# Slope term and causal mask of an attention moved from the vector engine into products on TensorE

## The chip, the core and the metric

One core of one Trainium2 chip runs the kernel. The metric is the device time of one execution in microseconds. A core has five engines that run their own instruction streams and meet at semaphores: TensorE (PE in the profile, with its weight loads shown apart as PEld), the vector engine (DVE), the scalar engine (ACT), GpSimd (POOL) and SyncE (SP), which issues transfers. Products land in PSUM, eight banks of 128 partitions by 512 fp32 numbers; everything else lies in SBUF.

## The reference, cut to what matters

The program is two transformer blocks on 512 tokens. The change touches two of the attentions of the first block and one neighbour. All three have eight heads, and all see the causal past only:

```
slopes = [2 ** -(h + 1) for h in range(8)]              # the two sparse/window branches only
# kinds 0 and 1 (selected blocks, window): queries and keys of 64 numbers a head
s = q @ k.T * 64 ** -0.5 - slopes[h] * (t - j)           # t: query, j: key
# kind 2 (latent attention): queries and keys of 96 numbers a head, no slope
s = (q_nope @ k_nope.T + q_rope @ k_rope.T) * 96 ** -0.5
p = softmax(where(j <= t, s, -1e30)) ; o = p @ v
```

With 512 tokens, eight blocks of 64 and sixteen to be chosen, the selection takes every block, and the window of 512 covers the whole past. So kinds 0 and 1 are both plain causal attentions with a slope term, over different keys and values. A softmax doesn't change when a number is added to a whole row of its scores, and so the term may be written as slopes[h] * j plus any constant of the row.

## The kernel before, in words

The first block runs in stages: projections (to 101 us of the profiled span), preparation of the attention's operands and the compressed attention (to 173 us), the attention stage (173 to 346 us), merge and feed-forward (to about 1000 us). The second block follows; from 1275 us on it streams the experts' weights.

**The attention stage** is cut into 48 units (`UNITS`, line 1600). A unit is one block of 128 queries (i = 0..3, so that nk = 128 * (i + 1) keys are seen), one kind, and two heads, pr and pr + 4 (hh = 0, 1). Units come in pairs, a long one and a short one: in the first 24 units i = 3 and i = 0 alternate ("(3,0)"), in the last 24 units i = 2 and i = 1 ("(2,1)"). In each half, eight units are kind 0, then eight kind 1, then eight kind 2. Each pair thus has five blocks of 128 keys a head, whichever half it is in.

For each unit, in order:

- TensorE (`scores`, lines 1710 to 1723) multiplies queries and keys, in fp32, into two PSUM banks, one a head. For kinds 0 and 1 the two heads lie in rows 0 to 63 and 64 to 127 of the array, so that their two products run side by side (line 1722); kind 2 uses 96 rows (line 1719). It waits until the exponentials of the unit before last have freed the banks.
- DVE (`mask_max`, line 2135) adds slope and mask in PSUM. For kinds 0 and 1 it is one instruction a head over all nk columns (line 2145), with a table of distances in which the future is -1e30; for kind 2 one instruction adds the 128-column diagonal table to both heads (line 2141). One reduction gives the negated row maxima of both heads (line 2149).
- ACT (`exps`, line 1884) computes the exponential of each head with that maximum as bias, into SBUF, and sums it.
- TensorE (`turn_probs`, line 1733) turns the probabilities in 128x128 pieces; DVE copies the first head's to SBUF (line 2157), ACT the second head's (line 1893).
- TensorE (`values`, line 1746) multiplies them with the values, 64 columns at a time, in fp32.

TensorE's order is: scores(u+1), turn(u), values(u-1). When a group of four units is through, DVE scales and gathers its output (`combine`, lines 2162 to 2171), in its own order, between two masks.

An fp32 product runs as two records in the trace, each with its weight load. Operands written as fp32r, a rounded format, run as one.

Of the kernel before, what the change touches and what calls it, by code (L numbers as in the profile page):

```python
# [119 lines left out]
CSTS = [("ident", 128), ("eps", 1), ("ones", 128), ("diag", 128), ("alibi", 512), ("inv_freq", 16), ("row_ok", 1),  # L120
# [14 lines left out]
cs_tr_ev cs_pv cs_o at_s at_max at_exp at_tr at_ev_dve at_ev_act at_pv at_o mg_sig mg_ev up_conv up_dve  # L135
# [28 lines left out]
def build(nc, W, EX, x, cols, csts, cmp_tab, pos, grows, pT, fconst, fwout, decay, frow, out):  # L164
    ctx = ExitStack()
    with ctx:
# [114 lines left out]

        rows_split = ar_r(25312, 2048).rearrange("p (u w c) -> p u w c", u=2, w=2)
# [1321 lines left out]
        def _(pe):  # L1604
# [103 lines left out]
            pe.wait_ge(S["cs_o"], 1)  # L1708

            def scores(u):  # L1710
                i, kind, pr, w = UNITS[u]
                nk = (i + 1) * P
                if u >= 2:
                    pe.wait_ge(S["at_exp"], 2 * (u - 1))
                for hh in range(2):
                    h = pr + 4 * hh
                    dst = pb[:, 2 * (u % 2) + hh, 0:nk]
                    if kind == 2:
                        last = nc.tensor.matmul(dst, qTm[0:QK, h, i * P:(i + 1) * P], kTm[0:QK, h, 0:nk], start=True, stop=True)
                    else:  # L1720
                        r = slice((h // 4) * 64, (h // 4) * 64 + 64)
                        last = nc.tensor.matmul(dst, qT[r, h % 4, i * P:(i + 1) * P], kvT[r, 2 + kind, 0:nk], start=True, stop=True)  # L1722
                last.then_inc(S["at_s"], 1)
# [89 lines left out]
        def _(act):  # L1813
# [60 lines left out]
            nc.scalar.activation(Pc[:, :, :, 0:31], Pc[:, :, :, 0:31], ACT.Exp).then_inc(S["cs_exp"], 1)  # L1874

            def exps(u):
                i, kind, pr, w = UNITS[u]
                nk = (i + 1) * P
                act.wait_ge(S["at_max"], u + 1)
                for hh in range(2):  # L1880
                    if u >= 2:
# [112 lines left out]
        def _(dve):  # L1994
# [136 lines left out]
            alibi = cs("alibi")  # L2131
# [3 lines left out]
            def mask_max(u):  # L2135
# [3 lines left out]
                dve.wait_ge(S["at_s"], u + 1)  # L2139
                if kind == 2:  # L2140
                    L(nc.vector.tensor_tensor(pb[:, b:b + 2, nk - P:nk], pb[:, b:b + 2, nk - P:nk],
                                              cs("diag").unsqueeze(1).broadcast_to([P, 2, P]), ALU.add))
                else:
                    for hh in range(2):
                        ins = nc.vector.scalar_tensor_tensor(out=pb[:, b + hh, 0:nk], in0=alibi[:, 512 - nk:512],  # L2145
# [334 lines left out]
```

## Time and profile before

| | us |
|---|---|
| median of 3 runs | 1809.21 |
| lowest and highest of them | 1800.8, 1812.97 |
| the profiled execution, its own time | 1807.25 |
| its span in the profile | 1805.5 |
| TensorE busy in the span | 1533.8 (85%) |
| DVE busy | 636.9 (35%) |
| mean granted TensorE clock | 0.93 of full |
| attention stage, first scores to the next stage's first turn | 173.6 to 345.8 |

The profile is of one execution. A granted clock of 1.00 is TensorE's full 2.4 GHz, 0.50 is 1.2 GHz. A record of a product lasts until its last number has left the array, so records of products that follow closely overlap, and the distance from one start to the next is what a product costs in a dense queue.

### The profile page before, as it was taken

What the parts mean: (1) busy time and instruction counts of PE and PEld (TensorE: products, weight loads), DVE (VectorE), ACT (ScalarE), POOL (GpSimd) and SP (SyncE); (2) the same over time, 40 slices, a digit from 0 to 9 for tenths busy, and PEclk for the clock granted to TensorE, in tenths of its full rate; (3) what the DMA queues carried; (4) which work ended last, traced back from release to release, by engine and by line L of the source; (5) the groups of instructions that cost most, each with busy time, mean ns of one, the idle gap of its engine ahead of it and who ended that gap; (6) DMA issues with size and microseconds to landing.
All of it is one profiled execution on the core that took longest, in us unless ns stands there. A gap on an engine that the chain in (4) does not pass through costs nothing.

```text
span 1805.5 us, 18567 instructions
## 1 busy us (share of the span) xinstructions
PE 1533.8 (85%) x7176; PEld 1038.8 (58%) x7177; DVE 636.9 (35%) x968; ACT 466.4 (26%) x798; POOL 464.4 (26%) x272
## 2 busy tenths in 40 slices
PE   7976898899979999999997899896687777877871
PEld 5954576788767888878866666466332222222320
DVE  3244667712345333332143778654300000000003
ACT  4231334432233333321134333322000000000001
POOL 4420000144334444444423363521010000010001
PEclk9986888999999999999999899997799999999996
DMA  7320000033232332323323222127499999999983
GB/s 278 105 71 35 1 1 1 1 94 100 87 93 82 101 98 94 97 90 95 94 80 105 76 82 68 50 109 287 177 427 427 428 427 426 426 426 423 424 352 147
DMA packets 47045, 315.24 MB, mean 175 GB/s; under 512 B 7344, under 2 KB 7344, under 8 KB 34560
## 3 DMA queue, kind: packets, MB, share of 16 engines
q1 hardware_dynamic: 37296, 286.80, 41.3%
q0 software_dynamic: 9104, 25.39, 3.9%
q10 hardware_dynamic: 576, 2.10, 0.3%
q8 instruction: 47, 0.77, 0.2%
q14 instruction: 22, 0.18, 0.0%
HBM read 307.97 MB, written 14.68 MB: 179 GB/s over the span
## 4 chain that ended last, share of the span: by engine, by line
PE 60%; DMA 18%; DVE 14%; issue 3%; ACT 2%; POOL 1%; SPq 0%; POOLq 0%; ACTq 0%; DVEq 0%
PE banks L353 22%; DMA arena<-experts 17%; PE banks L383 10%; PE banks L920 8%; PE banks L1776 3%; PE banks L363 2%; PE banks L831 1%; PE banks L1746 1%; DVE st L2149 1%; PE banks L688 1%; PE banks L1733 1%; PE banks L689 1%; DVE banks L2145 1%; PE banks L1722 1%; DVE arena_r L1580 1%
## 5 line engine op out<-in xcount | busy, mean ns | idle before, releaser
L331 POOL TENSOR_TENSOR arena_r<-ring,arena_r 128x1024 fp32r<-128x1024 f32 x143 | 353.2, 2472 | 747.1 <-ACT arena_r L316 747.1
L353 PE MATMUL banks<-hT_r,arena_r 128*128 128x512 f32 x1216 | 391.9, 392 | 8.7 <-POOL arena_r L331 4.3
L920 PE MATMUL banks<-ring,arena 128*64 128x512 f32 x768 | 246.0, 626 | 65.2 <-DMA arena<-experts 45.1
L353 PE MATMUL banks<-arena_r 128*128 128x512 f32 x800 | 291.7, 389 | 0.0
L316 ACT ACTIVATE arena_r<-ring 128x1024 fp32r<-128x1024 f32 x143 | 151.1, 1059 | 519.6 <-PE banks L353 316.9
L353 PEld LDWEIGHTS banks<-hT_r,arena_r 128*128 128x128 f32 x1216 | 228.4, 188 | 67.4 <-issue 9.2
L920 PEld LDWEIGHTS banks<-ring,arena 128*64 128x64 f32 x768 | 80.6, 144 | 218.4 <-issue 161.0
L383 PE MATMUL banks<-arena_r 128*128 128x512 f32 x784 | 187.4, 393 | 3.6 <-POOL arena_r L331 3.6
L383 PEld LDWEIGHTS banks<-arena_r 128*128 128x128 f32 x784 | 147.2, 188 | 38.3 <-POOL arena_r L331 5.4
L353 PEld LDWEIGHTS banks<-arena_r 128*128 128x128 f32 x800 | 150.3, 188 | 30.8
L942 PE MATMUL banks<-arena 128*64 128x512 f32 x512 | 118.5, 617 | 19.4 <-DMA arena<-experts 13.9
L920 PE MATMUL banks<-arena 128*64 128x512 f32 x256 | 130.8, 670 | 0.0
L587 POOL DMA_INDIRECT back<-arena,at_out x16 | 16.3, 1017 | 441.5 <-DVE arena L1384 229.4
L1379 DVE TENSOR_TENSOR arena<-arena,banks 128x512 f32<-128x512 f32 x16 | 11.0, 688 | 300.1 <-PE banks L920 300.1
L942 PEld LDWEIGHTS banks<-arena 128*64 128x64 f32 x512 | 40.3, 141 | 87.3 <-issue 74.6
L2236 DVE SCALAR_TENSOR_TENSOR arena<-banks,colt,arena 128x511 f32<-128x511 f32 x44 | 33.0, 750 | 151.6 <-ACT arena L1937 151.6
L1884 ACT ACTIVATE arena<-banks,st 128x512 f32<-128x512 f32 (+3 forms) x96 | 49.8, 525 | 107.8 <-DVE st L2149 107.7
L1733 PE MATMUL banks<-cst,arena 128*128 128x128 f32 x240 | 46.6, 315 | 21.8 <-ACT arena L1884 13.5
L1558 PE MATMUL banks<-cst,arena 128*128 128x128 f32 x192 | 30.8, 329 | 40.0 <-DVE arena L1532 25.9
L1746 PE MATMUL banks<-arena 128*128 128x64 f32 x480 | 64.3, 286 | 0.0
L1384 DVE COPY arena<-banks 128x512 f32<-128x512 f32 x16 | 11.1, 692 | 150.6 <-PE banks L942 150.6
L1746 PEld LDWEIGHTS banks<-arena 128*128 128x128 f32 x480 | 63.4, 208 | 0.0
(391 smaller groups left out, 1816.0 us busy)
## 6 DMA issues: line engine op xcount, KB each, us to landing
arena<-experts SPq DMA_DIRECT2D x48, 2048.0 KB, 21.2
ring<-experts SPq DMA_DIRECT2D x48, 2048.0 KB, 18.1
ring<-stream SPq DMA_DIRECT2D x163, 512.0 KB, 3.5
rows<-arena POOLq DMA_DIRECT2D x8, 512.0 KB, 6.8
arena<-back POOLq DMA_DIRECT2D x8, 512.0 KB, 7.3
grow<-grows POOLq DMA_DIRECT2D x5, 512.0 KB, 4.6
resid<-x ACTq DMA_DIRECT2D x4, 512.0 KB, 5.4
out<-arena POOLq DMA_DIRECT2D x4, 512.0 KB, 3.0
```

Source lines behind the costliest of these rows:

```text
L316: nc.scalar.activation(parts(name, m)[:, 0, :], tile(tile_n), ACT.Copy).then_inc(S["w_high"], 1)
L331: nc.gpsimd.tensor_tensor(w[:, 1, :], tile(tile_n), plain(w[:, 0, :]), ALU.subtract).then_inc(S["w_low"], 1)
L353: last = nc.tensor.matmul(pb[:, bank, :], w[:, a, k * P:(k + 1) * P], b[:, k, :], start=(k == 0 and part == 0), stop=(k == ND - 1 and part ...
L363: last = nc.tensor.matmul(pb[:, bank0 + i, 0:width], a[:, k, i * P:(i + 1) * P], w[:, v, q * width:(q + 1) * width], start=(k == 0 and par ...
L383: last = nc.tensor.matmul(pb[:, 2 * i + h, :], u[row], w[:, v, h * 512:(h + 1) * 512], start=(k == 0 and part == 0), stop=(k == K - 1 and ...
L920: last = nc.tensor.matmul(pb[r, bank, :], XT[:, k, r], chunk(c + e)[:, k * 512:(k + 1) * 512], start=(k == 0), stop=(k == ND - 1))
L942: last = nc.tensor.matmul(pb[r, 3 + h, :], hbT[:, k, r], chunk(4 + e)[:, k * D + h * 512:k * D + (h + 1) * 512], start=(k == 0), stop=(k = ...
L1733: last = nc.tensor.transpose(pb[:, 4 + hh, kt * P:(kt + 1) * P], Pr[:, u % 2, hh, kt * P:(kt + 1) * P], ident)
L1746: last = nc.tensor.matmul(pb[:, 6 + w % 2, h * DH:(h + 1) * DH], PTs[:, u % 2, hh, kt * P:(kt + 1) * P], v, start=(kt == 0), stop=(kt == i))
L1776: last = nc.tensor.matmul(pb[:, b + 2 + w, :], tw[:, u, (4 * w + k) * P:(4 * w + k + 1) * P], src[:, k, :], start=(k == 0 and part == 0), ...
L1884: nc.scalar.activation(Pr[:, u % 2, hh, 0:nk], pb[:, 2 * (u % 2) + hh, 0:nk], ACT.Exp, bias=nm[:, u % 2, hh:hh + 1], accum_out=sums[:, w, ...
L2236: L(nc.vector.scalar_tensor_tensor(out=c[:, 1:T], in0=u[:, 0:T - 1], scalar=col("w_conv", 2 * NF + m), in1=c[:, 1:T], op0=ALU.mult, op1=AL ...
```

## The change

Mask and slope are now part of the products that fill the banks. Four tables are rounded to fp32r by ACT after the compressed attention's exponential (`ident_r`, `diag_r`, `steps_r`, `slopes_r`). For kinds 0 and 1 a one-row product of the head's slope, repeated over 128 columns, with the key positions (0 for the last key, -1 for the one before) adds the slope term over all nk columns. For all kinds the product of the identity with the diagonal table adds the mask to the last 128 columns. DVE loses its additions, and its reduction becomes one a head, with a semaphore count a head from the product to the exponential.

```diff
--- before.py
+++ after.py
@@ -117,7 +117,7 @@
 N_COLS = _at
 
 
-CSTS = [("ident", 128), ("eps", 1), ("ones", 128), ("diag", 128), ("alibi", 512), ("inv_freq", 16), ("row_ok", 1),
+CSTS = [("ident", 128), ("eps", 1), ("ones", 128), ("diag", 128), ("steps", 512), ("slopes", 8), ("inv_freq", 16), ("row_ok", 1),
         ("giota", 4), ("eiota", 32), ("tri", 128), ("iota", 128), ("choice", 8), ("empty", 1), ("ecolumn", 32), ("erow", 32)]
 CST = {}
 _at = 0
@@ -132,7 +132,7 @@
 w_used w_high w_low rows_low hT_low oT_low h_high h_back cols_in ident_in x_in0 x_in1 x_in2 x_in3 tab_in g_in decay_in out_st
 dve_chain proj_fm_ev proj_mla_ev proj_v_ev cmp_blocks cmp_gelu cmp_kv cmp_ready ang_ready sin_ready mla_ms
 mla_rt mla_norm mla_tr mla_tr_ev mla_up q_ev kv_ev q_raw qk_tr qk_ev_act qk_ev_dve cs_mm cs_max cs_exp cs_tr
-cs_tr_ev cs_pv cs_o at_s at_max at_exp at_tr at_ev_dve at_ev_act at_pv at_o mg_sig mg_ev up_conv up_dve
+cs_tr_ev cs_pv cs_o at_tab at_s at_max at_exp at_tr at_ev_dve at_ev_act at_pv at_o mg_sig mg_ev up_conv up_dve
 up_gelu up_g ple_mm ple_ev pg_mm pg_sig in2_lin in2_conv in2_f z_ready f_in flt_mm flt_act flt_dve
 mixed tf_mm tf_act prod_ready y_ready xz_ready combined yh_dve pool_chain hn_sq_f hn_sq_h hn_ms hn_rt hn_y
 wo2_mm wo2_x rt_lg rt_g rt_d rt_exp rows_st xg_zero slot_ready slot_mm sel_ready rank_mm counts_out
@@ -279,6 +279,7 @@
         def ar_r(off, n):
             return arena_r[:, off:off + n]
 
+        ident_r, diag_r, steps_r, slopes_r = ar_r(25312, P), ar_r(25440, P), ar_r(25568, T), ar_r(26080, HEADS)
         rows_split = ar_r(25312, 2048).rearrange("p (u w c) -> p u w c", u=2, w=2)
         up_low = ar_r(18432, ND * T).rearrange("p (k t) -> p k t", k=ND)
 
@@ -1706,21 +1707,27 @@
 
 
             pe.wait_ge(S["cs_o"], 1)
+            pe.wait_ge(S["at_tab"], 4)
 
             def scores(u):
                 i, kind, pr, w = UNITS[u]
                 nk = (i + 1) * P
                 if u >= 2:
                     pe.wait_ge(S["at_exp"], 2 * (u - 1))
+                dst = [pb[:, 2 * (u % 2) + hh, 0:nk] for hh in range(2)]
                 for hh in range(2):
                     h = pr + 4 * hh
-                    dst = pb[:, 2 * (u % 2) + hh, 0:nk]
+                    r = slice(64 * hh, 64 * hh + 64)
                     if kind == 2:
-                        last = nc.tensor.matmul(dst, qTm[0:QK, h, i * P:(i + 1) * P], kTm[0:QK, h, 0:nk], start=True, stop=True)
+                        nc.tensor.matmul(dst[hh], qTm[0:QK, h, i * P:(i + 1) * P], kTm[0:QK, h, 0:nk], start=True, stop=False)
                     else:
-                        r = slice((h // 4) * 64, (h // 4) * 64 + 64)
-                        last = nc.tensor.matmul(dst, qT[r, h % 4, i * P:(i + 1) * P], kvT[r, 2 + kind, 0:nk], start=True, stop=True)
-                last.then_inc(S["at_s"], 1)
+                        nc.tensor.matmul(dst[hh], qT[r, pr, i * P:(i + 1) * P], kvT[r, 2 + kind, 0:nk], start=True, stop=False)
+                for hh in range(2):
+                    h = pr + 4 * hh
+                    if kind < 2:
+                        nc.tensor.matmul(dst[hh], slopes_r[0:1, h:h + 1].broadcast_to([1, P]), steps_r[0:1, T - nk:T],
+                                         start=False, stop=False)
+                    nc.tensor.matmul(dst[hh][:, nk - P:nk], ident_r, diag_r, start=False, stop=True).then_inc(S["at_s"], 1)
 
             def turn_probs(u):
                 i, kind, pr, w = UNITS[u]
@@ -1872,12 +1879,14 @@
 
             act.wait_ge(S["cs_max"], 1)
             nc.scalar.activation(Pc[:, :, :, 0:31], Pc[:, :, :, 0:31], ACT.Exp).then_inc(S["cs_exp"], 1)
+            for dst, name in ((ident_r, "ident"), (diag_r, "diag"), (steps_r, "steps"), (slopes_r, "slopes")):
+                nc.scalar.activation(dst, cs(name), ACT.Copy).then_inc(S["at_tab"], 1)
 
             def exps(u):
                 i, kind, pr, w = UNITS[u]
                 nk = (i + 1) * P
-                act.wait_ge(S["at_max"], u + 1)
                 for hh in range(2):
+                    act.wait_ge(S["at_max"], 2 * u + hh + 1)
                     if u >= 2:
 
                         act.wait_ge(S["at_tr"], 2 * (u - 2) + hh + 1)
@@ -2128,7 +2137,6 @@
                                     fac.unsqueeze(2).broadcast_to([P, 32, DH]), ALU.mult).then_inc(S["cs_o"], 1)
             dve.wait_ge(S["cs_o"], 1)
 
-            alibi = cs("alibi")
             rinv = st[:, 428:436]
             otmp = junk[:, 0:512]
 
@@ -2136,18 +2144,10 @@
                 i, kind, pr, w = UNITS[u]
                 nk = (i + 1) * P
                 b = 2 * (u % 2)
-                dve.wait_ge(S["at_s"], u + 1)
-                if kind == 2:
-                    L(nc.vector.tensor_tensor(pb[:, b:b + 2, nk - P:nk], pb[:, b:b + 2, nk - P:nk],
-                                              cs("diag").unsqueeze(1).broadcast_to([P, 2, P]), ALU.add))
-                else:
-                    for hh in range(2):
-                        ins = nc.vector.scalar_tensor_tensor(out=pb[:, b + hh, 0:nk], in0=alibi[:, 512 - nk:512],
-                                                             scalar=SLOPES[pr + 4 * hh], in1=pb[:, b + hh, 0:nk],
-                                                             op0=ALU.mult, op1=ALU.add)
-                    L(ins)
-                nc.vector.tensor_reduce(nm[:, u % 2, :], pb[:, b:b + 2, 0:nk], AX.X, ALU.max, negate=True)\
-                    .then_inc(S["at_max"], 1)
+                for hh in range(2):
+                    dve.wait_ge(S["at_s"], 2 * u + hh + 1)
+                    nc.vector.tensor_reduce(nm[:, u % 2, hh:hh + 1], pb[:, b + hh, 0:nk], AX.X, ALU.max, negate=True)\
+                        .then_inc(S["at_max"], 1)
 
             def copy_turned(u):
                 nk = (UNITS[u][0] + 1) * P
@@ -2304,7 +2304,8 @@
     p = np.arange(P)
     c = {"ident": np.eye(P), "eps": np.full((P, 1), EPS), "ones": np.ones((P, P)), "diag": np.where(p[None, :] <= p[:, None], 0.0, NEG)}
     dist = p[:, None] - (np.arange(512)[None, :] - 384)
-    c["alibi"] = np.where(dist >= 0, -dist, NEG)
+    c["steps"] = np.broadcast_to(np.arange(T) - (T - 1), (P, T))
+    c["slopes"] = np.broadcast_to(np.array(SLOPES), (P, HEADS))
     inv = (np.float32(10000.0) ** (-np.arange(0, 32, 2, dtype=f32) / f32(32))).astype(f32)
     c["inv_freq"] = np.broadcast_to(inv, (P, 16))
     c["row_ok"] = (p >= 31)[:, None]
```

**TensorE's order in the attention stage.** From the scores of one long unit (i = 3, kind 0 or 1) to those of the next short one (i = 0); 64-column products are the values, 128x128 ones from `cst` the turns. Before:

```order
L1722 MATMUL banks<-arena 128x512 [waits at_exp]
L1722 MATMUL banks<-arena 128x512
L1733 MATMUL banks<-cst,arena 128x128 [waits at_ev_dve,at_exp]
L1733 MATMUL banks<-cst,arena 128x128 [waits at_ev_act,at_exp]
L1746 MATMUL banks<-arena 128x64 [waits at_ev_dve]
L1746 MATMUL banks<-arena 128x64 x3
L1746 MATMUL banks<-arena 128x64 [waits at_ev_act]
L1746 MATMUL banks<-arena 128x64 x3
```

and with the change:

```order
L1724 MATMUL banks<-arena 128x512 [waits at_exp]
L1724 MATMUL banks<-arena 128x512
L1728 MATMUL banks<-arena_r 128x512
L1730 MATMUL banks<-arena_r 128x128
L1728 MATMUL banks<-arena_r 128x512
L1730 MATMUL banks<-arena_r 128x128
L1740 MATMUL banks<-cst,arena 128x128 [waits at_ev_dve,at_exp]
L1740 MATMUL banks<-cst,arena 128x128 [waits at_ev_act,at_exp]
L1753 MATMUL banks<-arena 128x64 [waits at_ev_dve]
L1753 MATMUL banks<-arena 128x64 x3
L1753 MATMUL banks<-arena 128x64 [waits at_ev_act]
L1753 MATMUL banks<-arena 128x64 x3
```

Four products stand between the scores and the turns, and they alternate between one row of the array (line 1728) and all 128 (line 1730). Nothing else moves.

**DVE's order at the same place**, from the mask of one long unit to that of the next; the 128x512 copy is the long unit's turned probabilities. Before:

```order
L2145 SCALAR_TENSOR_TENSOR banks<-cst,banks 128x512 [waits at_s]
L2145 SCALAR_TENSOR_TENSOR banks<-cst,banks 128x512
L2149 TENSOR_REDUCE st<-banks 128x2 [waits dve_chain]
L2157 COPY arena<-banks 128x128 [waits at_tr]
L2145 SCALAR_TENSOR_TENSOR banks<-cst,banks 128x128 [waits at_s]
L2145 SCALAR_TENSOR_TENSOR banks<-cst,banks 128x128
L2149 TENSOR_REDUCE st<-banks 128x2 [waits dve_chain]
L2157 COPY arena<-banks 128x512 [waits at_pv,at_tr]
```

and with the change:

```order
L2149 TENSOR_REDUCE st<-banks 128x1 [waits at_s] x2
L2157 COPY arena<-banks 128x128 [waits at_pv,at_tr]
L2149 TENSOR_REDUCE st<-banks 128x1 [waits at_s] x2
L2157 COPY arena<-banks 128x512 [waits at_pv,at_tr]
```

Two reductions of one head each take the place of two additions and one reduction.

## Rows read from the trace of the kernel before

**Rows 1.** Chain of waits, attention stage, 172 to 346 us: share by line.

```profile
by line: PE banks L1746 12.4%; DVE st L2149 12.2%; PE banks L1733 11.5%; DVE banks L2145 11.1%; issue 10.7%; PE banks L1722 10.6%; PE banks L1719 8.9%; ACT arena L1884 8.2%; ACT arena L1893 2.3%; DVE banks L2141 2.0%; DVE arena L2171 2.0%; 
```

**Rows 2.** Waits in that stretch: who for whom, us, times, longest.

```profile
ACT arena L1884 <- DVE st L2149: 107.7, 38, 16.6
PEld banks L1733 <- ACT arena L1884: 34.5, 48, 3.4
```

**Rows 3.** Busy time by stretch: length, engines, PEclk; stage, low-clock parts, one full.

```profile
173.20:345.80 172.60, 149.40 (x912) 113.46 (x912) 111.64 (x217) 70.09 (x240) 0.00 (x0) 0.87 0.00 1
173.20:183.50 10.30, 6.82 (x22) 3.67 (x23) 4.64 (x9) 2.74 (x9) 0.00 (x0) 0.50 0.00 0
200.50:204.00 3.50, 3.50 (x12) 2.12 (x12) 0.46 (x1) 1.15 (x5) 0.00 (x0) 0.51 0.00 0
214.20:221.00 6.80, 5.44 (x20) 3.64 (x21) 2.83 (x8) 2.91 (x10) 0.00 (x0) 0.50 0.01 2
231.30:244.90 13.60, 13.60 (x48) 10.76 (x49) 6.52 (x15) 3.95 (x15) 0.00 (x0) 0.50 0.00 0
299.50:309.80 10.30, 10.17 (x43) 8.24 (x44) 4.33 (x10) 2.91 (x10) 0.00 (x0) 0.50 0.01 2
246.00:299.00 53.00, 46.24 (x326) 35.02 (x324) 38.97 (x77) 24.39 (x83) 0.00 (x0) 1.00 0.00 1
```

**Rows 4.** Timeline of one pair: start us, us, engine, line, operation [idle before].

```profile
188.51 1.13 PE L1722 MATMUL banks<-arena 64*128 64x512 f32 x4
...
189.68 1.29 DVE L2145 SCALAR_TENSOR_TENSOR banks<-cst,banks 128x512 f32<-128x512 f32 x2 [1.66 <-PE banks L1722]
189.74 1.86 PEld L1746 LDWEIGHTS banks<-arena 128*128 128x128 f32 x16
...
191.01 1.22 DVE L2149 TENSOR_REDUCE st<-banks 128x2 f32<-128x1024 f32 x1
...
192.27 0.69 ACT L1884 ACTIVATE arena<-banks,st 128x512 f32<-128x512 f32 x1 [3.45 <-DVE st L2149]
...
192.87 0.42 DVE L2149 TENSOR_REDUCE st<-banks 128x2 f32<-128x256 f32 x1
...
193.10 0.66 PE L1733 MATMUL banks<-cst,arena 128*128 128x128 f32 x4 [0.94 <-ACT arena L1884]
...
194.03 0.63 PE L1733 MATMUL banks<-cst,arena 128*128 128x128 f32 x4 [0.27 <-ACT arena L1893]
```

**Rows 5.** Busy time of pairs: (3,0), (3,0) in kind 2, (2,1).

```profile
188.51:194.98 6.47, 5.26 (x40) 3.97 (x39) 4.23 (x8) 2.91 (x11) 0.00 (x0) 1.00 0.00 0
250.73:257.04 6.31, 5.90 (x39) 4.49 (x39) 3.31 (x6) 2.97 (x11) 0.00 (x0) 1.00 0.00 0
275.22:281.18 5.96, 5.26 (x40) 3.98 (x40) 4.23 (x8) 3.02 (x13) 0.00 (x0) 1.00 0.00 0
```

**Rows 6.** Busy time in the stretch before the attention's scores.

```profile
161.90:173.50 11.60, 7.90 (x24) 6.11 (x24) 5.38 (x6) 0.00 (x0) 0.00 (x0) 0.65 0.00 0
```

**Rows 7.** TensorE timeline where the shape of the array's use changes.

```profile
1012.63 0.40 PE L353 MATMUL banks<-hT_r,arena_r 128*128 128x512 f32 x1
1012.96 1.07 PE L706 MATMUL banks<-arena,colt 33*64 33x512 f32 x2
1013.96 0.50 PE L353 MATMUL banks<-hT_r,arena_r 128*128 128x512 f32 x1
1014.29 0.40 PE L353 MATMUL banks<-arena_r 128*128 128x512 f32 x1
```

**Rows 8.** Weight loads in the same view: scores of 512 columns, then turns.

```profile
251.05 0.19 PEld L1719 LDWEIGHTS banks<-arena 96*128 96x128 f32 x1 [0.24 <-issue]
251.48 0.19 PEld L1719 LDWEIGHTS banks<-arena 96*128 96x128 f32 x1 [0.24 <-issue]
251.91 0.14 PEld L1733 LDWEIGHTS banks<-cst,arena 128*128 128x128 f32 x1 [0.24 <-issue]
```

**Rows 9.** Chain of waits, merged: one-pass products of 512 columns.

```profile
404.87 10.99 PE banks L353 x48
```

## The prediction, made before the changed kernel was run

> **What bounds the kernel now.** The change touches the attention stage alone, so I read that stage and take the rest as it is. The chain of waits over it [rows 1] has no single owner: values, turns and scores on TensorE, additions (L2145) and reductions (L2149) on DVE, and the exponentials (L1884) take turns. The waits say who stands still: ACT waits 107.7 us for DVE's maxima, TensorE's weight loads 34.5 us for the exponentials [rows 2]. One pair of units in the timeline shows the loop [rows 4]. The scores of the long unit start at 188.51, DVE adds the slope from 189.68 (1.29 us), reduces from 191.01 (1.22 us), the exponential starts at 192.27, the turns at 193.10 and 194.03 after waits of 0.94 and 0.27 us. The next long scores start at 194.98: the pair takes 6.47 us [rows 5], and 2.5 us of that are DVE's.
>
> The reader should also see how little TensorE stands still. It is busy 5.26 of the 6.47 us, 5.90 of 6.31 in kind 2, and 5.26 of 5.96 in the second half's pairs [rows 5]. Over the stage it is busy 149.4 of 172.6 us [rows 3]. That is part clock: the granted clock is 0.50 in five stretches, together 44.5 us (10.3, 3.5, 6.8, 13.6 and 10.3), and 1.00 elsewhere [rows 3].
>
> **The change, part by part, for one pair at full clock.**
>
> *DVE* loses both additions, 1.29 us for the long unit. Its two reductions of one head cost hardly more than the one of both (1.22 us): I take 1.3. The first exponential may start after the first reduction, half way. The chain from scores to next scores thus loses 1.29 us and some 0.6 more, and would fall to about 4.9 us, if the products added nothing. So does DVE's gathering of a finished group fall behind TensorE's work; I put no price on it beside the sum below.
>
> *TensorE's own work* is then late next. It is 5.26 us a pair less what is only the tail of the last product ahead of its two waits, some 0.15 us each (a record of 0.39 for a product that costs 0.23 [rows 7, 9] has such a tail): I take 5.0. In kind 2, 5.90 less 0.3: 5.6. To this the change adds:
>
> - Slope products: a one-pass product of 512 columns costs 10.99/48 = 0.23 us [rows 9]. Long unit of (3,0): 2 x 0.23. With 384 and 256 columns I take 0.17 and 0.12 in proportion, with 128 columns the price of a weight load, 1.86/16 = 0.12 [rows 4].
> - Mask products, 128 columns: no row shows a one-pass product so short. From below a quarter of 0.23, 0.06; from above the four passes of plain fp32, 2 x 0.43 x 128/512 = 0.21 [rows 8]. I take the load's 0.12: the load is the nearest row, as the turns and values run at it.
> - A change of the array's shape. Scores use 64 rows for a head, slope products one row, mask products and turns 128. The nearest row is an fp32 product of 33 rows and 64 columns among full ones [rows 7]: from 1012.63 to 1014.29 are 1.66 us, in which two full products (0.46) and two passes' records of 0.43 [rows 8] (0.86) account for 1.32. The two changes of shape cost 0.34, 0.17 each. A unit of kinds 0 and 1 has two now (into the scores, out of them) and five with the change: three more, 0.51. Bounds: 0, if one row of the array can be used without a change of shape, and 0.17 each; I take 0.17, the nearest row; the ends leave 16 x 1.02 = 16 us between them. The Trainium skill, TensorEngine Tiling (Array Packing), Key Properties, says that a change of tiling mode drains TensorE and that 32 rows are a mode of their own; no row here shows the 32-row mode, while the rows above show a drain for another. By the rule the 0.17 stands; without it the time would be rival A's.
>
> Sum a pair: (3,0), long 2 x 0.23 + 2 x 0.12 + 0.51 = 1.21, short 4 x 0.12 + 0.51 = 0.99, together 2.2, and with 5.0 it is 7.2. (2,1): 2 x 0.17 + 2 x 0.12 + 0.51 = 1.09 and 0.99, 2.1, so 7.1. Kind 2 has no slope and, with 96 rows, no change of shape (the first turn's load follows the last score's at 0.43 like the ones before [rows 8]): 4 x 0.12 = 0.5, so 6.1. So TensorE's work passes the shortened chain everywhere, and also the 6.47 and 5.96 us of now: **the bound moves to TensorE**, and its 1.2 us of idle time a pair are bought with 2.1 us of work.
>
> *The stage at full clock:* 8 pairs x 7.2 + 8 x 7.1 + 8 x 6.1 = 163.2 us, plus 4 us to fill and empty the loop (scores, maxima and exponentials of the first unit; values and gathering of the last): 167.
>
> *The clock.* The stage begins at 0.50 after preparations in which TensorE waits a lot; that stays, and 10.3 us at half clock lose 5: 172, against 172.6 now. Further low stretches are the open term. Today there are 34.2 us of them [rows 3]. As long as TensorE bounds, each costs half its length. I count a third of them, 11 us, since TensorE's gaps at DVE's work, 23 of the stage's 172.6 us, go; not none, since at 231.30 to 244.90 TensorE was busy 13.60 of 13.60 us and still at 0.50 [rows 3]. That adds 5.5: **177 to 178, 5 us more than now.**
>
> *ACT's four table copies* (128, 128, 512 and 8 columns, under 1.7 us by the 0.69 of its 512-column exponential [rows 4]) go where ACT does nothing for 11.6 us [rows 6]: nothing. If that cover were gone they would cost their 1.7. The finer semaphores cost nothing beside products of 0.12.
>
> Made against the profiled execution (1807.25): 1812. The median of the runs is 1809.2, 2 us above it, so between the two bases I forecast **1813 us**. A measurement here can tell about 1% (18 us) from no change: below 1791 is faster, above 1827 slower.
>
> **The rivals.**
>
> A, *the shape is free*: the one-row products don't drain the array, and the 16 pairs lose 1.02 each, 16 us. Then the stage is 161, and the time 1797; 1791 if the clock is full besides. For it: nothing in the trace has such a small shape. Against: in the one place of the rows where the shape changes twice, it costs 0.34. Chance 0.12.
>
> B, *the clock stays full after the start*: 172, the time 1808. For it: from 246 to 299 it stayed full though TensorE was busy only 46.24 of 53.00 us [rows 3]. Against: the fully busy low stretch at 231.30. The Trainium skill, TensorE: Matmul & The Clock Gate, Loop structure matters more than you think, has it that products kept back to back stay warm. That stretch disagrees; by the rule the time would be this rival's 1808. Chance 0.2.
>
> C, *slower*: TensorE falls to half clock and stays there, since a pair that TensorE bounds takes 14 us at half clock, so that the same products lie thinner in time and don't bring the clock back. Today's 34.2 us of low stretches would cost 17 instead of the 5.5 I count: 189, the time 1824; it decides against the kernel by over 1% from some 40 us on, and 60 us give 1837. For it: the fully busy stretch that stayed low for 13.6 us, in kind 2 where TensorE has the most work a pair now; and one row's product is little work for its columns. Against: today's clock falls in a stage with gaps, and they go. Chance 0.25.
>
> D, *the mask products cost four passes*, 0.09 more each: 96 of them, 9 us: 1822. Chance 0.05, in the range.
>
> My forecast has the rest, 0.38. The range 1797 to 1832 takes in A at today's clock, B, D, and C up to 50 us of low clock. Faster by over 1%: 0.06, half of A. Slower by over 1%: 0.16, the greater half of C and what D adds. Within: 0.78.
>
> **What would show it.** TensorE's idle time for ACT (the 34.5 us) gone, and ACT's wait for DVE replaced by work; pairs of kinds 0 and 1 at 7.1 to 7.2 us where the clock is 1.00, and of kind 2 at 6.1; in the timeline a start-to-start distance of about 0.4 from a slope product of 512 columns to its mask product, against 0.23 if A is right. Pairs below 6.3 us would make the sum wrong; low stretches of over 40 us would decide for C, under 12 us for B.

## The result, and the profile after it

| | before | after |
|---|---|---|
| median of the runs, us | 1808.74 (1800.57 to 1812.97, 13 runs) | **1819.99** (1816.06 to 1828.25, 13 runs) |
| ratio, 95% interval | | 1.0083 [1.0063, 1.0104] |
| profiled execution: its own time, span, us | 1807.25, 1805.5 | 1818.82, 1817.1 |
| start to first score product, us | 173.6 | 175.4 |
| attention stage, us | 172.3 | 170.7 |
| of it at a granted clock of 0.50, us | 44.5 | 17.1 |
| end of the stage to the end, us | 1459.7 | **1471.0** |

The kernel became 0.8% slower, 7 us above the forecast of 1813 and inside its range. The table says where. The stage, from its first score product to the first transposition of the merge behind it, did not get longer in the profile, though with 27 us less of low clock in it. The net loss lies behind it, in code that the change doesn't touch.

First the stage. The chain of waits over it, shares by line, after the change:

```profile
by line: PE banks L1753 28.1%; PE banks L1740 15.5%; PE banks L1724 14.5%; PE banks L1728 13.0%; PE banks L1730 11.2%; PE banks L1722 8.8%; issue 1.4%; DVE arena L2135 1.3%; DVE st L2149 0.8%; DVE arena L2171 0.8%; DVE junk L2166 0.8%; DVE 
```

In [rows 1] DVE's additions and maxima (L2145, L2149) and ACT's exponentials held almost a third of the chain. Now 91% of it is TensorE: values L1753, turns L1740, scores L1724 and L1722, slope L1728, mask L1730. The waits of the same stretch (engine, line, whom for: us, times, longest) put it the other way round. The exponentials, L1884 before, stand on L1893 now:

```profile
ACT arena L1893 <- DVE st L2149: 101.9, 49, 13.0
DVE st L2149 <- PE banks L1730: 76.3, 48, 4.4
```

ACT still waits 102 us for the maxima (107.7 in [rows 2]), but the maxima themselves now wait 76 us for the mask product. Of TensorE's 34.5 us of waiting for the exponentials 0.4 are left. Busy time by stretch (window, its length, then busy us of PE, PEld, DVE, ACT, POOL with their counts, PEclk, DMA share, GB/s): the stage, its one low stretch, the rest, then a pair of (3,0), one of kind 2 and one of (2,1), each from the first score product of its long unit to that of the next:

```profile
175.40:346.10 170.70, 169.18 (x1073) 131.64 (x1073) 82.72 (x184) 72.78 (x240) 0.00 (x0) 0.95 0.00 1
178.10:195.20 17.10, 17.10 (x64) 12.70 (x64) 4.65 (x10) 6.16 (x19) 0.00 (x0) 0.50 0.00 0
195.20:346.10 150.90, 149.40 (x1003) 117.63 (x999) 77.30 (x173) 66.57 (x221) 0.00 (x0) 1.00 0.01 1
216.19:223.32 7.13, 7.13 (x47) 5.34 (x47) 4.78 (x11) 3.72 (x14) 0.00 (x0) 1.00 0.00 1
249.72:255.61 5.89, 5.89 (x44) 4.93 (x44) 2.60 (x6) 2.90 (x11) 0.00 (x0) 1.00 0.01 3
268.50:275.62 7.12, 7.12 (x48) 5.34 (x47) 3.67 (x8) 3.47 (x12) 0.00 (x0) 1.00 0.02 3
```

TensorE is busy 169.2 of 170.7 us (149.4 of 172.6 in [rows 3]), and all of each pair. The pairs of kinds 0 and 1 got longer, 7.13 and 7.12 us for 6.47 and 5.96 [rows 5], those of kind 2 shorter, 5.89 for 6.31. The timeline of one long unit shows what fills them:

```profile
223.32 1.13 PE L1724 MATMUL banks<-arena 64*128 64x512 f32 x4
224.38 0.50 PE L1728 MATMUL banks<-arena_r 1*128 1x512 f32 x1
224.81 0.33 PE L1730 MATMUL banks<-arena_r 128*128 128x128 f32 x1
225.06 0.50 PE L1728 MATMUL banks<-arena_r 1*128 1x512 f32 x1
225.49 0.33 PE L1730 MATMUL banks<-arena_r 128*128 128x128 f32 x1
225.66 0.41 PE L1740 MATMUL banks<-cst,arena 128*128 128x128 f32 x2
```

From a slope product's start to its mask product's are 0.43 us, and from the mask product to the next slope product 0.25. A one-pass product of 512 columns has 0.23 of work [rows 9], so 0.2 of each step lie between products of different shape. From 224.38 to 225.66 the additions take 1.28 us of TensorE in this unit. In the short unit before it they take 0.93:

```profile
221.01 0.32 PE L1728 MATMUL banks<-arena_r 1*128 1x128 f32 x1
...
221.94 1.06 PE L1740 MATMUL banks<-cst,arena 128*128 128x128 f32 x8
```

Now the code behind the stage. From 560 to 790 us TensorE does nothing but one-pass products of 512 columns (L353 before, L354 after), and the chain of waits of either kernel is one piece (start, us, what). Before:

```profile
559.95 230.07 PE banks L353 x1015
```

After:

```profile
559.87 230.30 PE banks L354 x987
```

That is 226.7 ns a product before and 233.3 after, for the same instruction on the same shapes. The diff doesn't touch it. What it moves is the place of its operands: the table of constants grew from 1279 to 1287 columns of 4 bytes (steps 512 and slopes 8 for 512 of the slope table), and the arena, which is allocated behind it and holds the rounded weights, begins 32 bytes further in each partition. `hT_r`, from which two of three of these products read, is allocated ahead of the table and stays. Not every one-pass product got slower: the 528 of line 383 (384 after) that follow, with both operands in the arena, take the same time in either kernel:

```profile
792.40:917.70 125.30, 123.39 (x530) 99.13 (x528) 28.08 (x48) 28.92 (x34) 50.80 (x21) 1.00 0.29 89
```

and after:

```profile
801.40:926.70 125.30, 123.43 (x529) 99.15 (x527) 28.02 (x47) 28.89 (x34) 50.74 (x21) 1.00 0.29 89
```

### The profile page after: what moved, and what is told of

It reads as the page before. It is cut to its first block, busy times and chain, and to the rows that moved or that the text cites. A ratio compares the mean times of both kernels' runs of the same rounds, so it can differ in the third digit from the quotient of the medians.

```text
span 1817.1 us, 18906 instructions
## 1 busy us (share of the span) xinstructions
PE 1566.6 (86%) x7336; PEld 1059.1 (58%) x7337; DVE 608.6 (33%) x936; ACT 470.5 (26%) x802; POOL 463.6 (26%) x272
## 4 chain that ended last, share of the span: by engine, by line
PE 65%; DMA 18%; DVE 11%; issue 3%; ACT 1%; POOL 1%; SPq 0%; POOLq 0%; DVEq 0%; ACTq 0%
PE banks L354 23%; DMA arena<-experts 17%; PE banks L384 10%; PE banks L921 8%; PE banks L1753 3%; PE banks L1783 3%; PE banks L364 2%; PE banks L1740 1%; PE banks L832 1%; PE banks L1724 1%; PE banks L1728 1%; PE banks L689 1%; PE banks L690 1%; PE banks L1730 1%; DVE arena_r L1581 1%
## 5 line engine op out<-in xcount | busy, mean ns | idle before, releaser
L354 PE MATMUL banks<-hT_r,arena_r 128*128 128x512 f32 x1216 | 398.6, 397 | 8.9 <-DVE arena_r L1581 6.1
L921 PE MATMUL banks<-ring,arena 128*64 128x512 f32 x768 | 242.1, 620 | 63.1 <-DMA arena<-experts 43.9
L354 PE MATMUL banks<-arena_r 128*128 128x512 f32 x800 | 296.0, 395 | 0.0
L354 PEld LDWEIGHTS banks<-hT_r,arena_r 128*128 128x128 f32 x1216 | 228.7, 188 | 73.2 <-issue 8.8
L354 PEld LDWEIGHTS banks<-arena_r 128*128 128x128 f32 x800 | 150.0, 187 | 35.0
L1893 ACT ACTIVATE arena<-banks,st 128x512 f32<-128x512 f32 (+3 forms) x96 | 50.3, 526 | 102.3 <-DVE st L2149 101.9
L2149 DVE TENSOR_REDUCE st<-banks 128x1 f32<-128x512 f32 (+3 forms) x96 | 45.1, 489 | 77.9 <-PE banks L1730 76.3
L1559 PE MATMUL banks<-cst,arena 128*128 128x128 f32 x192 | 31.0, 332 | 40.2 <-DVE arena L1533 26.4
L1753 PE MATMUL banks<-arena 128*128 128x64 f32 x480 | 60.8, 276 | 0.0
L1753 PEld LDWEIGHTS banks<-arena 128*128 128x128 f32 x480 | 59.4, 198 | 0.0
```

The costliest lines, as they stand in the source:

```text
L354: last = nc.tensor.matmul(pb[:, bank, :], w[:, a, k * P:(k + 1) * P], b[:, k, :], start=(k == 0 and part == 0), stop=(k == ND - 1 and part ...
L921: last = nc.tensor.matmul(pb[r, bank, :], XT[:, k, r], chunk(c + e)[:, k * 512:(k + 1) * 512], start=(k == 0), stop=(k == ND - 1))
L1753: last = nc.tensor.matmul(pb[:, 6 + w % 2, h * DH:(h + 1) * DH], PTs[:, u % 2, hh, kt * P:(kt + 1) * P], v, start=(kt == 0), stop=(kt == i))
L1893: nc.scalar.activation(Pr[:, u % 2, hh, 0:nk], pb[:, 2 * (u % 2) + hh, 0:nk], ACT.Exp, bias=nm[:, u % 2, hh:hh + 1], accum_out=sums[:, w, ...
L2149: nc.vector.tensor_reduce(nm[:, u % 2, hh:hh + 1], pb[:, b + hh, 0:nk], AX.X, ALU.max, negate=True)\
```

## Experiments

The theories were two. **Place**: the loss outside the stage comes from where the arena begins, whatever the attention does. **Array**: inside the stage, the one-row slope products cost little by their columns and much by the changes of shape. The rivals: something of the new attention slows what follows; and a product of few columns has a floor that makes the same sum without a drain. The per-head maximum and the clock were tested beside them. Ratios are of the runs' medians; the last four columns, in us, are of one profiled execution each (r1's was the slowest of its ten):

| run | ratio to before, 95% interval | arena moved, bytes | to the stage | stage | of it low | behind it |
|---|---|---|---|---|---|---|
| before | 1 | 0 | 173.6 | 172.3 | 44.5 | 1459.7 |
| after | 1.0083 [1.0063, 1.0104] | 32 | 175.4 | 170.7 | 17.1 | 1471.0 |
| p1_before_plus8 | 1.0048 [1.0029, 1.0067] | 32 | 177.7 | 164.8 | 23.8 | 1469.9 |
| p2_after_plus8 | 1.0129 [1.0096, 1.0162] | 64 | 177.4 | 176.8 | 30.7 | 1477.5 |
| p3_after_plus8_full | 0.9982 [0.9966, 0.9997] | 64 | 175.9 | 151.2 | 10.2 | 1476.3 |
| p4_after_plus8_grouped | 1.0056 [1.0039, 1.0073] | 64 | 179.1 | 157.3 | 10.2 | 1476.9 |
| q1_after_same | 1.0026 [1.0005, 1.0046] | 0 | 174.7 | 176.7 | 30.7 | 1460.6 |
| q2_after_same_full | **0.9859** [0.9838, 0.9880] | 0 | 175.4 | 147.3 | 0 | 1460.1 |
| q3_same_full_onemax | 0.9898 [0.9874, 0.9921] | 0 | 179.4 | 153.4 | 10.2 | 1461.3 |
| q4_before_headmax | 0.9931 [0.9913, 0.9948] | 0 | 176.7 | 155.9 | 23.8 | 1458.3 |
| r1_after_plus24 | 1.0013 [0.9993, 1.0034] | 128 | 179.3 | 176.8 | 30.7 | 1463.0 |
| r2_same_filled | 1.0028 [0.9995, 1.0060] | 0 | 178.1 | 175.3 | 27.3 | 1463.4 |
| r3_before_filled | 0.9989 [0.9968, 1.0009] | 0 | 173.4 | 173.0 | 44.4 | 1459.0 |

The last column goes by the bytes of the fourth, not by the kernel: 1458 to 1463 at 0, 1470 and 1471 at 32, 1476 to 1478 at 64, 1463 at 128. Each of these figures holds 150 to 194 us of low clock, most of it later than 1200 us, so a difference of 3 us says little. Free of it is the stretch from the first of the 1056 products of line 353 or 354 to the first of line 383 or 384 behind them, at a granted clock of 1.00 in all runs: it takes 241.6 or 241.7 us at 0 bytes (seven kernels), 246.2 (p1) and 248.5 (the changed kernel) at 32, 249.6 or 249.7 at 64, 243.9 at 128.

### The place of the arena

**p1_before_plus8**, the kernel before with eight unused columns:

```diff
-... ("alibi", 512), ("inv_freq", 16), ("row_ok", 1),
+... ("alibi", 512), ("inv_freq", 16), ("row_ok", 1), ("pad", 8),
```

> The kernel before with eight unused columns more in its table of constants, so that everything allocated after that table (above all the arena, where the rounded weights lie) starts 32 bytes further on, as in the changed kernel. No instruction of the work is changed. Theory 'place': the changed kernel's loss outside the attention stage comes from where the arena lies; then the one-pass products of line 353 go from 227 to 232-235 ns start to start, and the time rises by 10 to 13 us, ratio 1.006 to 1.007, with the attention stage unchanged at 172 us. Rival 'clock or transfers': the loss comes with the attention's products in some other way; then the products stay at 227 ns and the ratio is 1.000.

1815.75 us against 1806.65. Its chain from 560 to 790 us:

```profile
559.82 230.19 PE banks L353 x996
```

231.1 ns a product: eight columns that nobody reads make the kernel before 0.5% slower, 10 us behind the stage, with nothing of the new attention in it. Inside the stage this execution was 7.5 us shorter than that of before, with 23.8 us of low clock for 44.5; that the columns do this is not shown. The changed kernel's products, at the same 32 bytes, take 233.3 ns, 2 more than p1's; that part is open.

**p2_after_plus8**, the same eight columns added to the changed kernel, 64 bytes in all.

> The changed kernel with eight unused columns more in the table, so that the arena lies 64 bytes further on than in the kernel before. Theory 'place' with 64 bytes as the unit: products of line 354 back at 227 ns, time 1807 to 1810, ratio 0.998 to 1.001: what is left is the attention stage. If the unit is 128 bytes: still 232 to 235 ns and the ratio stays at 1.008. Rival 'clock or transfers': as the changed kernel, 1820.

1833.68 us, above all of the expected times. Behind the stage 18 us are lost, more than with 32 bytes; 64 bytes are no multiple that helps. The stage is the longest of all, with 30.7 us at a clock of 0.50.

**q1_after_same**, the change without the slopes' columns; ACT makes the slopes from one number of the steps, and the arena stands where it stood before:

```diff
-            for dst, name in (..., (steps_r, "steps"), (slopes_r, "slopes")):
+            for dst, name in (..., (steps_r, "steps")):
                 nc.scalar.activation(dst, cs(name), ACT.Copy).then_inc(S["at_tab"], 1)
+            for h in range(HEADS):
+                nc.scalar.activation(slopes_r[:, h:h + 1], cs("steps")[:, T - 2:T - 1], ACT.Copy, scale=-SLOPES[h])...
```

> The changed kernel with its arena exactly where it lies in the kernel before: the eight slopes don't come from the table of constants but are made by ACT from one number of the steps table (eight one-column copies, in the same idle stretch). Theory 'place': the one-pass products of the later stages are back at 227 ns, and what is left is the attention stage, which took 170.7 us in the changed kernel against 172.3: time 1805 to 1812, ratio 0.998 to 1.003. Rival: the 32 bytes are not the cause, the time stays at 1820.

1814.13 us (1806.28 to 1819.24). In its chain of waits, the same one-pass products:

```profile
412.06 10.99 PE banks L354 x48
```

That is the 10.99 of [rows 9] to the digit (the changed kernel has 11.09 there), and what follows the stage takes 1460.6 us. The change as it was meant costs 0.3% [0.05, 0.5]; the other half per cent of the 0.83 is the arena's place. Busy time of its stage and of the low stretch in it:

```profile
174.70:351.40 176.70, 175.24 (x1072) 135.88 (x1072) 82.68 (x184) 72.74 (x240) 0.00 (x0) 0.91 0.00 1
177.20:207.90 30.70, 30.70 (x112) 22.49 (x112) 7.66 (x17) 9.43 (x29) 0.00 (x0) 0.50 0.00 1
```

**r1_after_plus24**, the changed kernel with 24 unused columns, 128 bytes in all:

```diff
-... ("slopes", 8), ("inv_freq", 16), ("row_ok", 1),
+... ("slopes", 8), ("inv_freq", 16), ("row_ok", 1), ("pad", 24),
```

> The changed kernel with 24 unused columns more in its table of constants, so that the rounded weights begin 128 bytes further than before the change, not 32 or 64. Theory 1, what counts is where an operand begins within 128 bytes: the one-pass products of the projections and of the feed-forward come back to 227 ns from start to start, the time outside the attention stage is that of the kernel before, and the kernel takes 1806 to 1819 us. Theory 2, the rate falls with the table's growth itself or with the arena's distance: 230 to 238 ns, and 1816 to 1834 us.

1811.26 us. TensorE's timeline, three products for each block of weights (two read `hT_r`, one the arena alone):

```profile
600.74 0.62 PE L354 MATMUL banks<-hT_r,arena_r 128*128 128x512 f32 x2
601.20 0.39 PE L354 MATMUL banks<-arena_r 128*128 128x512 f32 x1
601.42 0.62 PE L354 MATMUL banks<-hT_r,arena_r 128*128 128x512 f32 x2
601.88 0.39 PE L354 MATMUL banks<-arena_r 128*128 128x512 f32 x1
602.11 0.39 PE L354 MATMUL banks<-hT_r,arena_r 128*128 128x512 f32 x1
```

Six products from 600.74 to 602.11: 228 ns. With the table longer than ever the time is nearly back, which excludes the table's length as such. "Nearly": the 1056 products take 243.9 us for 241.7 in q1. So the start within 128 bytes is what counts most, not all.

### What the slope product costs TensorE

**p3_after_plus8_full**, against p2: the slope product on all 128 rows, each with 1/128 of the slope, so that it has the mask product's shape:

```diff
-nc.tensor.matmul(dst[hh], slopes_r[0:1, h:h + 1].broadcast_to([1, P]), steps_r[0:1, T - nk:T], ...
+nc.tensor.matmul(dst[hh], slopes_r[:, h:h + 1].broadcast_to([P, P]), steps_r[:, T - nk:T], ...
```

> As the one before, but the slope product uses all 128 rows of the array (each row holds the slope over 128, and the key positions stand in every row), so that it has the shape of the mask product. Theory 'shape': three changes of shape fewer in each unit of kinds 0 and 1, 0.17 us each, 0.51 a unit: pairs of kinds 0 and 1 go from 7.13 to about 6.1 us at full clock, the stage loses 16 us, ratio about 0.991 against the kernel before. Rival 'the price is the products themselves or their number': pairs stay at 7.1 us and the time stays at that of the run before.

1804.03 us, 30 us less than p2 for 128 times the arithmetic in the slope products. Pairs take 6.15 and 6.03 us, kind 2 stays at 5.88. In the profiles the stage is 25.6 us shorter. It has 20.5 us less of low clock, which by half the length is 10 of them; the other 15 are work, 16 expected.

**p4_after_plus8_grouped**, against p2: both slope products, then both mask products.

```diff
                     if kind < 2:
                         nc.tensor.matmul(dst[hh], slopes_r[0:1, ...
+                for hh in range(2):
                     nc.tensor.matmul(dst[hh][:, nk - P:nk], ident_r, diag_r, ...
```

> As the second run, but both heads' slope products stand first and then both mask products: three changes of shape a unit in place of five. Theory 'shape': two changes fewer a unit, 0.34, and the identity's second load overlaps: pairs of kinds 0 and 1 at about 6.4 to 6.5 us, the stage 10 to 11 us shorter than in the second run. Rival 'products': no change, since the same products run.

1816.31 us. Its TensorE, in the unit that answers to the one shown above:

```profile
208.34 0.72 PE L1728 MATMUL banks<-arena_r 1*128 1x512 f32 x2
209.00 0.44 PE L1731 MATMUL banks<-arena_r 128*128 128x128 f32 x2
209.27 0.40 PE L1741 MATMUL banks<-cst,arena 128*128 128x128 f32 x2
```

From the first slope product to the turns 0.93 us, for 1.28. The same instructions in another order, two changes of shape fewer a unit. So the cost is in the changes and not in the one-row product: a floor for short products would leave 1.28. By pairs of (3,0): 7.13 with five changes a unit, 6.51 with three, 6.15 with two. That makes 0.62/4 = 0.155 and 0.36/2 = 0.18 us a change, and 0.98/6 = 0.16 over both. By pairs of (2,1), 7.12, 6.45 and 6.03, it is 0.17, 0.21 and 0.18. These 0.16 to 0.18 us agree with the Trainium skill, TensorEngine Tiling (Array Packing), Key Properties, that changing the tiling mode drains TensorE; the page has no price for it.

**q2_after_same_full**, both repairs together: q1's arena and p3's full slope product.

> As the one before, with the slope product on all 128 rows (slope over 128 in each). Both causes of the loss taken away: pairs of kinds 0 and 1 at 6.0 to 6.2 us, stage 154 to 156 us, the rest as in the kernel before: 1789 to 1793, ratio 0.989 to 0.992. If the place is not the cause: 1804, as the third run.

**1784.64 us, 1.4% faster than before**, 35 us below the change as made and 4 below the range expected. Against q1 it is 29.5 us. In the profiles 15.4 of these are q1's 30.7 us of low clock, by half their length, and 14 are work. Busy time of its stage and of one pair, then the long unit in TensorE's timeline:

```profile
175.40:322.70 147.30, 145.52 (x1072) 121.20 (x1072) 80.02 (x184) 70.46 (x240) 0.00 (x0) 1.00 0.01 1
210.66:216.80 6.14, 6.14 (x47) 5.05 (x46) 2.69 (x6) 3.00 (x11) 0.00 (x0) 1.00 0.01 1
```

```profile
211.72 0.50 PE L1728 MATMUL banks<-arena_r 128*128 128x512 f32 x1
...
212.05 0.22 PE L1730 MATMUL banks<-arena_r 128*128 128x128 f32 x1
...
212.11 0.44 PE L1728 MATMUL banks<-arena_r 128*128 128x512 f32 x1
...
212.39 0.22 PE L1730 MATMUL banks<-arena_r 128*128 128x128 f32 x1
...
212.45 0.39 PE L1740 MATMUL banks<-cst,arena 128*128 128x128 f32 x2
```

0.73 us from the first slope product to the turns, for 1.28: three changes less, 0.18 each. The products and their weight loads alternate as in the changed kernel and only the rows differ, so it is not the alternation of weights that costs. A mask product after a product of its own shape takes 0.06 us, a quarter of the 0.23 for 512 columns. The stage has no low stretch at all.

### The maximum per head

**q4_before_headmax**, the kernel before with only the maxima and their counts split by head:

```diff
-                act.wait_ge(S["at_max"], u + 1)
                 for hh in range(2):
+                    act.wait_ge(S["at_max"], 2 * u + hh + 1)
...
-                nc.vector.tensor_reduce(nm[:, u % 2, :], pb[:, b:b + 2, 0:nk], ...
+                for hh in range(2):
+                    nc.vector.tensor_reduce(nm[:, u % 2, hh:hh + 1], pb[:, b + hh, 0:nk], ...
```

> The kernel before with only the second part of the change: one maximum a head, the first exponential waits for its own head alone; slope and mask stay on DVE. TensorE's products are those of before. Theory: DVE's chain bounds there, so the first exponential and the first turns start about 0.55 us sooner in long units, but the second head's maximum comes no sooner: pairs of (3,0) 6.47 to 6.2 or less, the stage 5 to 10 us shorter at equal clock, ratio 0.994 to 0.998. Rival: the second head's exponential sets the pair, so nothing: 1.000.

1796.63 us, 0.7% faster. The timeline of its long unit:

```profile
203.67 1.29 DVE L2145 SCALAR_TENSOR_TENSOR banks<-cst,banks 128x512 f32<-128x512 f32 x2 [1.60 <-PE banks L1722]
...
205.00 1.29 DVE L2150 TENSOR_REDUCE st<-banks 128x1 f32<-128x512 f32 x2
...
205.72 0.69 ACT L1884 ACTIVATE arena<-banks,st 128x512 f32<-128x512 f32 x1 [2.92 <-DVE st L2150]
```

The exponential starts 0.72 us after the reductions, 1.26 before [rows 4]; both reductions together take 1.29 for 1.22. Pairs fall from 6.47 to 5.94 and from 5.96 to 5.56 us, those of kind 2 from 6.31 to 5.78, but in the second half only from 6.36 to 6.10 and from 6.53 to 6.45. In the profiles the stage is 16.4 us shorter, with 20.7 us less of low clock. That is at most 10 by half its length, which leaves at least 6 for the reordering; how the medians' 12.9 us divide is not shown.

**q3_same_full_onemax**, q2 with one reduction for both heads again:

> As the second of this call, but with one reduction for both heads as in the kernel before; the change's second part undone. Theory: TensorE bounds, DVE has slack, so the row maximum per head is worth nothing: within 2 us of the second run. Rival: the earlier first exponential is what lets TensorE run dense: 5 to 14 us slower (0.2 to 0.6 us a pair).

1792.71 us, 8 us above q2, which by the number is the rival's range. But most pairs of kinds 0 and 1 are q2's own, 6.15 and 6.03 us, where the rival had 0.2 to 0.6 more in each; those of kind 2 in the first half take 6.02 for 5.89. In the profiles the stage is 6.1 us longer, 5 of them by 10.2 us of low clock, and 4.0 us more lie ahead of the stage, in code that is the same, with 44.7 us of low clock for 34.1. So the clock makes most of the difference in these two executions, and about 1 us is left for the maximum. Where DVE bounds the pair, the per-head maximum is worth 0.4 to 0.5 us in most pairs; where TensorE does, next to nothing.

### The clock at the start of the stage

In each kernel with one-row products between the mask products, the low stretch begins 2.4 to 4.3 us after the stage's start and lasts 17.1 us in the changed kernel's profile, 27.3 to 30.7 us in p2, q1, r1 and r2. Two kernels tried whether TensorE's waits just ahead of the stage make it.

**r2_same_filled** and **r3_before_filled**, q1 and the kernel before with dummy products in the last two of these waits:

```diff
+            def fill(n, bank):
+                for _ in range(n):
+                    nc.tensor.matmul(pb[:, bank, 256:512], ident, cs("steps")[:, 0:256], start=True, stop=True)
...
+            fill(3, 3)
             pe.wait_ge(S["cs_tr_ev"], 1)
...
+            fill(5, 7)
```

> The change with the arena at its place of before (the slopes made by ACT), and dummy products of 256 columns in TensorE's last two waits ahead of the attention stage (three in 1.4 us, five in 2.4 us); they write banks that nobody reads, and add nothing to the result. Theory 1, the 30.7 us at a granted clock of 0.50 at the start of the stage come from the waits just ahead of it: they shrink to 10.3 us or vanish, and the kernel takes 1797 to 1806 us. Theory 2, TensorE's waits have no part in it (the stage's own mix of products sets the clock): a low stretch of 17 to 31 us stays and the time is 1808 to 1816 us.

> The kernel before with the same eight dummy products in TensorE's last two waits ahead of the stage. If the waits ahead of it make the low stretch at its start (10.3 us in the profile), that stretch goes and 2 to 5 us with it: 1804 to 1807 us; the other four low stretches stay. If the waits have no part in it: 1809 us, within 2 us.

r2, ahead of the stage (waits filled) and in its low stretch:

```profile
167.60:178.10 10.50, 10.18 (x41) 8.63 (x41) 5.48 (x6) 1.71 (x12) 0.00 (x0) 0.78 0.00 0
182.40:209.70 27.30, 27.30 (x99) 20.03 (x99) 6.40 (x13) 7.55 (x25) 0.00 (x0) 0.50 0.00 1
```

r3, at the start of its stage:

```profile
177.20:190.90 13.70, 12.87 (x50) 9.42 (x50) 5.80 (x12) 5.77 (x19) 0.00 (x0) 0.50 0.01 1
```

TensorE was busy 10.2 of the 10.5 us ahead of the stage, and the clock fell to 0.50 some microseconds later all the same, for 27.3 us in which it was busy without a gap. In r3 the stretch at the start is 13.7 us, for 10.3. r2's time is q1's (1.0028 for 1.0026), r3's is that of before. So filling the waits just ahead of the stage does not take the stretch away. The earlier wait of 6.1 us (for the compressed attention's exponential) was left as it is, since all banks are in use there; it may still have a part.

## Why the prediction came out as it did

**The bound moves to TensorE: right.** TensorE fills 7.13 of 7.13 us of a pair, and DVE's 2.5 us on the path of [rows 4] are off it. DVE's part was sized well too: q4 gives 0.53 for the half-way start in a pair of (3,0), forecast 0.6, and 0.40 in one of (2,1). The shortened chain was added up wrongly: 6.47 less 1.29 and 0.6 is 4.6, not 4.9. Nothing hangs on it, since TensorE's 7.13 is far above either.

**The price of the products: right for kinds 0 and 1** (7.2 and 7.1 forecast, 7.13 and 7.12 measured), and by its own terms: 0.17 us for a change of shape was an estimate from one place in another stage [rows 7], and p3, p4 and q2 give 0.16 to 0.18 in (3,0). Rival A (shape free) fell. Two errors cancel inside the pair. The additions take 1.28 and 0.93 us, and less the one change a unit that was there before (0.17) that is an estimate of 1.9 new, for 2.2; a mask product was priced 0.12 where q2 shows 0.06 in a long unit. The 5.0 of other work was low by about as much. In kind 2 the sum said 6.1; the pairs take 5.88 to 5.98, one 6.35.

**The stage at full clock: 5 us too long.** 170.7 less half of 17.1 are 162.2 us, forecast 167. Of the difference about 1 is kind 2 (5.97 a pair on average), under 1 the other pairs, and 3 the 4 us for filling and emptying the loop, which took about 1.

**The clock: the forecast lay between the executions.** It had 10.3 us at the start and 11 later, costing 10.5. The profile after has one stretch of 17.1 us (8.6), q1, p2 and r1 one of 30.7 (15.4). Rival C's mechanism is seen there: q1's second and third pair, wholly at half clock, take 12.8 us each with TensorE busy throughout, and the clock comes back only in the fourth. Its size of over 40 us was never reached. Rival B is refuted for this order of products; q2, with the same work in one shape, has it as B said, yet q3 and p3 show that 10.2 us can come back. So the stage by itself costs q1 0.3%, 4.6 us in the medians: the forecast of 5 us more for the stage holds for the change as meant, by two errors that cancel, 5 us of work too much and up to 5 of low clock too little.

**"Take the rest as it is": wrong, and it is what the forecast missed.** A table that grows by eight columns looked like nothing to cost. It moved every buffer behind it by 32 bytes, and the one-pass products of line 353 run at 231 to 233 ns instead of 227: 11 us behind the stage. p1 shows it without the change, q1 shows the change without it, and r1 most of the way back. Without this term the forecast would have been 1 us off the median of q1; with it, it was 7 us low. That it was no more is luck: in the profiled execution the stage took 170.7 us for the 177 to 178 forecast, which hid more than half of these 11 us.

**ACT's table copies, the finer semaphores: nothing,** as forecast, as far as the runs resolve: q1 makes eleven copies there, the changed kernel four, and q1's stage starts 1.1 us after that of before, the changed kernel's 1.8.

## What to carry to other kernels

Before adding short products to TensorE, write down the row and column shape of each neighbour: here a change of shape cost 0.16 to 0.18 us, as much as 384 columns of work, and padding one row to 128 made the product cheaper (q2, 1.4% faster than before, where the one-row form lost; about half of q2's gain over q1 is clock). When a change adds or resizes a buffer, look at where the ones allocated behind it begin: a few bytes can cost more than the edit gives. And an improvement of the waiting chain (the per-head maximum, 0.7% alone) is worth its price only as long as that chain bounds: try it alone before joining it with something that moves the bound.

## What the runs showed of the hardware that was not expected

- One-pass products of 512 columns on line 353 (354) took 227 ns from start to start with the arena where it was, 231 to 233 ns with it 32 bytes further, 234 with it 64 further, and 228 to 229 with it 128 further. Most of them read one operand from `hT_r`, which did not move; the 528 of line 383 (384) with both operands in the arena took 125.3 us before and after. So not every product suffers, and the operands' distance from each other may count, but the merge's products (L1776, L1783 after), all in the arena, went from 228 to 230. Which operand does it was not separated.
- The granted clock stayed at 0.50 for 17 to 31 us while TensorE was busy without a gap, in five kernels, with and without waits just ahead. The Trainium skill, TensorE: Matmul & The Clock Gate, Loop structure matters more than you think, has it that products kept back to back stay warm; these stretches disagree. That p4 and p3 had 10.2 us, from the stage's first product on, and q2 none goes with fewer changes of shape, but what in them decides is open.
- A slope product on one row is not cheaper than on 128 rows: 0.43 us to the mask product behind it with a change of shape, 0.28 to 0.33 without one (q2).
